# Two transformer blocks, fp32 on one core: the mixers' projections take their high-part products first, and low parts of the weights move one step later

## The reference

```python
for l in range(DEPTH):                                   # first block, DEPTH = 2
    x = x + 0.5 * swiglu(rms_norm(x, ffn1_norm[l]), ffn1_w_in[l], ffn1_w_out[l])
    x = x + mixer(rms_norm(x, mix_norm[l]), mix_w_in[l], ...)   # local attention + Fourier mix, gated
    x = x + 0.5 * swiglu(rms_norm(x, ffn2_norm[l]), ffn2_w_in[l], ffn2_w_out[l])
...
for l in range(DEPTH):                                   # second block
    x = x + 0.5 * swiglu_ffn(x, ffn1_norm[l], ffn1_w_gu[l], ffn1_w_down[l])
    h = rms_norm_2(x, mix_norm[l])
    x = x + hybrid_mixer(h, w_in[l], w_gate[l], ...)
    x = x + 0.5 * swiglu_ffn(x, ffn2_norm[l], ffn2_w_gu[l], ffn2_w_down[l])
```

```python
g_a, g_b, g_c = jnp.split(jax.nn.sigmoid(h @ w_gate), 3, axis=-1)
merged = g_a * (o_a @ w_br_a) + g_b * (o_b @ w_br_b) + g_c * (o_c @ w_br_c)
return merged @ w_out
```

## Time and profile before

| | |
|---|---|
| time, median of 3 runs | 2309.7 us (2308.81 to 2310.12) |
| profiled execution | 2308.23 us, of which the span is 2306.4 |
| TensorE busy | 2286.8 us (99%), 16096 matmuls |
| TensorE weight loads | 2089.4 us (91%) |
| VectorE busy | 1835.0 us (80%) |
| ScalarE busy | 1151.5 us (50%) |
| HBM read | 405.23 MB, 176 GB/s over the span |

### The profile page before, as it was taken

One profiled execution on the slowest core, in us unless ns is written; L12 is line 12 of the kernel. 1 busy time (PEld: TensorE's weight loads), 2 busy tenths in 40 slices (PEclk: granted clock), 3 DMA queues, 4 the chain that ended last, 5 costly groups with the idle time before them and its releaser, 6 DMA issues.

```text
span 2306.4 us, 42275 instructions
## 1 busy us (share of the span) xinstructions
PE 2286.8 (99%) x16096; PEld 2089.4 (91%) x16096; DVE 1835.0 (80%) x2987; ACT 1151.5 (50%) x1533; POOL 4.8 (0%) x10
## 2 busy tenths in 40 slices
PE   8999999999999999999999999999999999999999
PEld 7998999999998999999999888999999998889998
DVE  7788568778888558877878887887798788878877
ACT  5445465445444565434443676654354347656443
POOL 0000000000000000000000000000000000000000
PEclk9999999999999999999999999999999999999999
DMA  6555445555555435555556433455555554334654
GB/s 242 187 191 202 152 149 192 191 187 169 191 191 201 165 132 190 200 191 164 191 185 198 173 140 121 165 192 184 187 175 191 190 170 173 125 123 168 214 187 131
DMA packets 76383, 407.61 MB, mean 177 GB/s; under 512 B 9216, under 2 KB 9872, under 8 KB 43776
## 3 DMA queue, kind: packets, MB, share of 16 engines
q1 hardware_dynamic: 75936, 405.78, 51.6%
q0 software_dynamic: 208, 0.49, 0.1%
q10 hardware_dynamic: 144, 0.04, 0.0%
HBM read 405.23 MB, written 1.05 MB: 176 GB/s over the span
## 4 chain that ended last, share of the span: by engine, by line
PE 94%; DVE 4%; issue 1%; ACT 1%; DMA 1%; SPq 0%; DVEq 0%; ACTq 0%
PE ps_proj L571 14%; PE ps_aux L571 14%; PE ps_y L213 10%; PE ps_y L215 10%; PE ps_y L214 10%; PE ps_proj L576 7%; PE ps_aux L576 7%; PE ps_proj L213 5%; PE ps_proj L215 5%; PE ps_proj L214 5%; PE ps_y L1663 1%; PE ps_aux L1696 1%; PE ps_y L1674 1%; DVE w_lo_front L111 1%; DVE w_lo_back L111 0%
## 5 line engine op out<-in xcount | busy, mean ns | idle before, releaser
L111 DVE TENSOR_TENSOR w_lo_front<-w_raw_front,w_hi_front 128x2048 fp32r<-128x2048 f32 x242 | 553.3, 2286 | 60.3 <-ACT w_hi_front L89 58.1
L89 ACT CAST w_hi_front<-w_raw_front 128x2048 fp32r<-128x2048 f32 x242 | 462.0, 1909 | 190.7 <-PE ps_aux L571 161.1
L571 PE MATMUL ps_proj<-xt_lo_hi,w_hi_front 128*128 128x512 f32 x1408 | 511.8, 394 | 10.0 <-DVE w_lo_front L139 9.0
L571 PE MATMUL ps_aux<-xt_lo_hi,w_hi_front 128*128 128x512 f32 x1408 | 511.7, 394 | 1.1 <-DVE w_lo_front L139 1.1
L213 PE MATMUL ps_y<-hidden_lo,w_hi_back 128*128 128x256 f32 x1408 | 396.9, 282 | 0.8 <-DVE hidden_lo L761 0.3
L215 PE MATMUL ps_y<-hidden_hi,w_hi_back 128*128 128x256 f32 x1408 | 396.5, 282 | 0.0
L214 PE MATMUL ps_y<-hidden_hi,w_lo_back 128*128 128x256 f32 x1408 | 396.0, 281 | 0.0
L576 PE MATMUL ps_aux<-xt_lo_hi,w_lo_front 128*128 128x256 f32 x1408 | 371.6, 283 | 0.0
L576 PE MATMUL ps_proj<-xt_lo_hi,w_lo_front 128*128 128x256 f32 x1408 | 369.2, 282 | 0.0
L89 ACT CAST w_hi_back<-w_raw_back 128x1024 fp32r<-128x1024 f32 x252 | 265.0, 1052 | 190.6 <-PE ps_y L215 148.7
L701 ACT ACTIVATE silu_gate<-silu_gate 128x256 f32<-128x256 f32 x176 | 73.7, 419 | 493.6 <-DVE silu_gate L738 493.6
(11 more groups left out here) (395 smaller groups left out, 3703.8 us busy)
## 6 DMA issues: line engine op xcount, KB each, us to landing
w_raw_front<-in_stream SPq DMA_DIRECT2D x252, 1024.0 KB, 4.9
w_raw_back<-in_stream SPq DMA_DIRECT2D x252, 512.0 KB, 3.7
m_rel_bias<-in_rel_bias SPq DMA_DIRECT2D x2, 2048.0 KB, 8.8
m_params<-in_params SPq DMA_DIRECT2D x2, 656.0 KB, 4.3
x<-in_x SPq DMA_DIRECT2D x4, 256.0 KB, 6.1
w_raw_front<-in_stream SPq DMA_DIRECT2D x2, 512.0 KB, 6.0
out<-x SPq DMA_DIRECT2D x3, 256.0 KB, 2.2
m_dft_time<-in_dft_t POOLq DMA_DIRECT2D x1, 256.0 KB, 3.6
```

Of the source, the lines that this page charges most:

```text
L89: self.nc.scalar.copy(self.hi[part][:, parity], self.raw[part][:, parity]).then_inc(self.hi_done[part], 1)
L111: eng.tensor_tensor(self.lo[part][:, parity], self.raw[part][:, parity], self.hi[part][:, parity].bitcast(F32), ALU.subtract).then_inc(sel ...
L571: return nc.tensor.matmul(bank[:], hi[:, cols], s.xlh[:, k].rearrange("p j t -> p (j t)"), start=k == 0, stop=k == KD - 1)
```

## The change

Three edits:

1. `project` takes its 24 matmuls in another order. First come, for the 8 pieces, high weight by low activation and high weight by high activation, behind a wait for the high part alone (`hi_done`); then a wait for the low part (`split`), and the 8 matmuls of low weight by high activation. The matmuls are the same, in number and in size.
2. In the loop of mixer 2, `BACK_AT` and with it `FRONT_AT` are one step later: the low parts of the backs of slots 10, 11, ... at steps 1, 4, ..., and of the fronts of slots 11, 12, ... at steps 2, 5, ....
3. The copy of gate 3 on ACT goes from ahead of the three query copies to between the second and the third.

```diff
--- before.py
+++ after.py
@@ -916,15 +916,24 @@
 
 def project(s, w, base, slot0, q, out, xn=None):
 
-    hi, lo = w.chunk(s.nc.tensor, base, slot0 + q // 3, q % 3)
+    nc, pe = s.nc, s.nc.tensor
+    slot, c = slot0 + q // 3, q % 3
+    hi, lo = w.parts(slot, c)
+    if c != 1:
+        pe.wait_ge(w.hi_done[c // 2], base + slot + 1)
     for k in range(KD):
         if xn is not None and k % 2 == 0:
             mark, layer = xn
-            mark.need(s.nc.tensor, layer, "xn_ready", k // 2 + 1)
-        cols = slice(k * P, (k + 1) * P)
-        last = product(s.nc, out, (hi[:, cols], lo[:, cols]), (s.nh[:, k], s.nl[:, k]),
-                       k == 0, k == KD - 1)
-    w.taken(last, q % 3)
+            mark.need(pe, layer, "xn_ready", k // 2 + 1)
+        part = hi[:, k * P:(k + 1) * P]
+        nc.tensor.matmul(out, part, s.nl[:, k], start=k == 0, stop=False)
+        nc.tensor.matmul(out, part, s.nh[:, k], start=False, stop=False)
+    if c != 1:
+        pe.wait_ge(w.split[c // 2], base + slot + 3)
+    for k in range(KD):
+        last = nc.tensor.matmul(out, lo[:, k * P:(k + 1) * P], s.nh[:, k], start=False,
+                                stop=k == KD - 1)
+    w.taken(last, c)
 
 
 def wide_part(s, w, base, slot0, q0, j, banks, xh, xl, n=None):
@@ -1327,7 +1336,7 @@
 MERGED_LOWS = {1: 0, 2: 1, 5: 2, 7: 3}
 PCT_AT = 3
 SORTED = 2
-BACK_AT = {0: 10, **{step + 1: P2_GATE[g] // 3 + 1 for step, g in GATE_AT.items()
+BACK_AT = {1: 10, **{step + 2: P2_GATE[g] // 3 + 1 for step, g in GATE_AT.items()
                      if P2_GATE[g] % 3 == 2}}
 FRONT_AT = {step + 1: slot + 1 for step, slot in BACK_AT.items()}
 
@@ -1844,9 +1853,10 @@
             last = nc.scalar.copy(m.kbd[rows, j0:j1, e], s.py[b][rows, at:at + (j1 - j0) * T]
                                   .rearrange("p (a t) -> p a t", a=j1 - j0))
         mark.inc(last, "kT_ready")
-    w.wait_taken(act, base, slot0 + P2_GATE[3] // 3, P2_GATE[3] % 3)
-    mark.inc(nc.scalar.copy(m.gate[3][:, 0:T], s.pj[1][:, 0:T]), "gate_ready")
     for c3, bank in enumerate((3, 0, 1)):
+        if c3 == 2:
+            w.wait_taken(act, base, slot0 + P2_GATE[3] // 3, P2_GATE[3] % 3)
+            mark.inc(nc.scalar.copy(m.gate[3][:, 0:T], s.pj[1][:, 0:T]), "gate_ready")
         need("qT_done", c3 + 1)
         mark.inc(nc.scalar.copy(m.qT[:, 2 * c3:2 * c3 + 2].rearrange("p a t -> p (a t)"),
                                 s.py[bank][:]), "qT_ready")
```

## The result

| | before | changed |
|---|---|---|
| median of 20 runs | 2309.57 us (2308.57 to 2310.34) | 2312.97 us (2310.57 to 2314.09) |
| ratio | | 1.0014, interval 1.0008 to 1.0021 |
| profiled execution | 2308.23 us | 2313.06 us |

The changed kernel is 3.4 us slower, a ratio of 1.0014, within the 0.2% that was called no difference. The interval excludes 1, so the direction is measured: slower, as forecast (2311.5). Its runs also spread over 3.5 us instead of 1.8.

A forecast was written before the change was run, and what follows sets the result against it. TensorE, busy for 99% of the span, was taken as the bound. The terms 0 + 1.4 + 0.45 + 0 gave +1.85 us, on the median of 2309.7 a forecast of 2311.5, range 2306 to 2316.

The forecast's parts named there:

- The projections' order: In all 96 projections: the reordered matmuls stay 0.12 us apart and a met second wait costs nothing; 0 us.
- the third rival: In the projections: using the same stationary tile twice is cheaper, saving up to 10 us, 2302 us in all; chance 0.05.
- Both stalls: Loop steps 2 and 3: TensorE's waits behind VectorE's low parts, costing 0.70 and 0.57 us, both go.
- The lead is given back through the late back load, and 0.7 more: Loop step 4: slot 12's back load, 2.33 us later, delays pcT; the 1.2 us lead goes, +0.7 a layer, +1.4 in sum.
- Gate 7's wait for the same low part: Loop step 3: gate 7's projection now meets the front's low part late, costing up to 0.1 us.
- The later slots: Each third loop step: the chain from low part through load, cast and gate copy again delays TensorE; +0.45 us.
- Gate 3's copy: Ahead of the loop, among the query copies: moving it is worth 0, at best -0.37 us in each of two layers.
- The second rival: In the loop: slower load transfers cost TensorE their excess at every slot, 4.8 us on top of 1.4, 2316; chance 0.10.

The follow-up runs named there:

- The run with the early load: Changed kernel with both first low parts at the end of step 1 and later ones at their old steps: 2309.72 us against 2309.63 before, ratio 0.9999.
- the one with the moved copy: Changed kernel with ScalarE's copy of pcT moved from step 4 to ahead of gate 7's cast in step 3: 2310.36 us against 2309.22 before, ratio 1.0006.
- the run with the first pair alone: Changed kernel with only the first pair of low parts one step later, the later ones at their old steps: 2311.56 us against 2309.22 before, ratio 1.0011.
- nine copies: Kernel before with nine more copies of pcT ahead of the one TensorE waits for, in each layer: 2315.1 us against 2309.34, ratio 1.0026.

## Why the prediction was right, and what it left out

- **The projections' order costs nothing: right.** 2309.15 against 2309.22 alone, and the spacing stayed 0.12 us. The repeated stationary tile is loaded again and saves nothing, so the third rival falls. The Trainium skill, "TensorE: Matmul & The Clock Gate", "Step-by-step: what each phase is for", says that a load apart from the matmul lets one load once and multiply repeatedly; this code makes no use of that: the trace shows a load for each matmul, 0.12 us apart like the matmuls.
- **Both stalls go: right**, 0.71 and 0.57 us in layer 0 (0.70 and 0.57 said).
- **The lead is given back through the late back load, and 0.7 more: right.** Shifted by 1.33 us (the offset of +1.42 ahead of the loop less the 0.09), the issue was put at 1384.03 (it came at 1384.04), `pcT` at 1391.20 (1391.26), its use at some 1391.3 (1391.30). At the first use of `pcT` the loops had lost 0.6 and 1.02 us against 2 x 0.7. The 0.4 more of layer 1 comes in with the front's low part: in layer 1 it is 4.85 us later (1985.73, 1990.58), 2.65 past the offset of 2.20 there, and in layer 0 3.67 later, 2.24 past the offset. VectorE's work in layer 1 is behind by about that difference from step 0 on, and what makes it so is not shown. Gate 7's wait for the same low part (0.25 us idle at 1992.93, put at up to 0.1) adds nothing to the sum, since the wait for `pcT` behind it takes it in. The run with the early load and the one with the moved copy show that it is this chain.
- **The later slots, +0.45: wrong in place.** In the changed kernel they cost 0.15 us in layer 0 and nothing in layer 1, for the wait for pcT has made TensorE late enough. So it is in part luck that the waits come to 1.8 us where the sum said 1.85: 0.45 was put where 0.15 is, and layer 1 took 0.3 more than its 0.7. The term is real where that wait is gone (1.14 us at gate 12 in layer 0).
- **Gate 3's copy, 0: right**: the wait that it could have changed is 0.49 to 0.58 us in the two profiles of the changed kernel against 0.49, and the time doesn't show it.
- **What was missing: the clock.** The sum of the waits is 1.8 us; the medians differ by 3.4. The rest is the low clock behind the wait, some 1.6 us each time that it comes, which no term and no rival had. It came behind five of the eight waits of this kind in the four profiles that have them (two of the changed kernel, the run with the first pair alone, that with nine copies). I had put the new wait into the sum as a wait alone. The Trainium skill, "TensorE: Matmul & The Clock Gate", under "Why this matters for your kernels", advises against idle gaps between bursts of matmuls, for the clock falls after them; it names longer gaps than these. In kind the trace agrees, and on the length the trace decides: a granted clock of 0.50 behind 1.90 us of idle time. Runs without a fall show the waits alone: the nine of the changed kernel with a granted clock of 1.000, both sets together, have a median of 2311.4, the sixty of the kernel before in the sets beside them 2309.2, 2.2 apart, near the sum of 1.85. Under 1.000 it is 22 runs of 31 against 36 of 96, with medians of 2313.5 and 2310.0.
- **The second rival (the loads' way on each slot, 2316)** didn't happen: the load took 5.62 us.

## What to carry to other kernels

A low part, or any work that frees a buffer, does two things: it makes its result, and it lets the next transfer start. Moved later it can take a stall away and still lose, because the transfer that it holds back comes out at another place, in front of an in-order engine with something due behind it. Look for what is queued behind the waiting instruction and move that ahead (here one 0.38 us copy and one cast); and give two edits that lean on each other, like an order that asks later and a table that delivers later, a run each.

And a wait put on TensorE is not only its length: a wait of 1.9 us that took the place of two of half a microsecond brought, in five of the eight cases in the profiles, a stretch at the low clock that cost nearly as much again.

## What the runs showed of the hardware

TensorE's granted clock fell from the 2.4 GHz to the 1.2 GHz level behind some waits of 1.8 to 1.9 us and not behind others, for something over 3 us each. It fell behind those of 1.76 and 1.89 (second profile of the changed kernel), 1.90 (first profile, layer 1), 1.91 (first pair alone, layer 1) and 1.86 us (nine copies, layer 0), and not behind those of 1.86, 1.88 and 1.83 us in the other layer of the last three. So the length of the wait alone does not decide. Behind the waits of 1.2 and 1.4 us it did not fall in the profile. In the window that ends ahead of the use of `pcT` and in the next, in which the fall at 2001.4 us lies, TensorE was busy for 0.99 and 1.11 of 2.00 us.

A fall puts TensorE back by some 1.6 us. Over a whole run one or two falls show as a granted clock of 0.999, so that figure does not say where they were: of the 96 runs of the kernel before, which has no such wait, 36 have it too.

The clock also fell where TensorE did not wait long. In 6 of the 13 profiles, whatever the edit, it fell at 1094 us in a feed-forward, with TensorE busy for all of the windows around it. What the engine did there is, in the first profile of the changed kernel, 16 matmuls of two columns each:

```profile
1091.30 1.84 PE L540 MATMUL ps_y<-m_scores,squares 128*128 128x2 f32 x16
```

In two more (the tables alone at 1981.66, both low parts early at 1978.44) it fell just behind the start of layer 1's loop, after 0.52 us of idle time and 16 matmuls of 32 columns in 1.94 us. All 13 profiles have these instructions in both places; what brings a fall in some executions alone stays open. A busy TensorE is no sign that its clock stays up.
